# A feed-forward phase on one core: a bank copied for two late readers, last norm's weights loaded and used elsewhere, held sums ahead of the gated product

## What is computed

```python
def conv_ffn(x, w_up, ffn_conv_w, ffn_conv_b, w_down):
    u = causal_depthwise_conv(x @ w_up, ffn_conv_w, ffn_conv_b)   # width 3
    g = u[..., :D_FF]            # D_FF = 2816
    v = u[..., D_FF:]
    return (jax.nn.silu(g) * v) @ w_down

x = layer_norm(DEEPNORM_ALPHA * x + y, ln1_g[l], ln1_b[l])
y = conv_ffn(x, w_up[l], ffn_conv_w[l], ffn_conv_b[l], w_down[l])
x = layer_norm(DEEPNORM_ALPHA * x + y, ln2_g[l], ln2_b[l])
```

## Time and profile before

| what | value |
|---|---|
| median of 3 runs | 1924.68 us (1923.73 to 1924.71) |
| the profiled execution, time | 1924.79 us |
| the profiled execution, span | 1923.1 us, mean granted PE clock 0.990 |
| PE busy | 1869.6 us, 97% |
| DVE busy | 1472.9 us, 77% |
| ACT busy | 939.1 us, 49% |
| POOL busy | 213.5 us, 11% |
| DMA | 153 GB/s over the span |
| chain that ended last | PE 70%, DVE 8%, ACT 2%, DMA 2% |

### The profile page before, as it was taken

One profiled execution on the slowest core, in us unless ns is written; L12 is line 12 of the kernel. 1 busy time (PEld: TensorE's weight loads), 2 busy tenths in 40 slices (PEclk: granted clock), 3 DMA queues, 4 the chain that ended last, 5 costly groups with the idle time before them and its releaser, 6 DMA issues.

```text
span 1923.1 us, 26236 instructions
## 1 busy us (share of the span) xinstructions
PE 1869.6 (97%) x8722; PEld 1557.5 (81%) x8722; DVE 1472.9 (77%) x1931; ACT 939.1 (49%) x1598; POOL 213.5 (11%) x307
## 2 busy tenths in 40 slices
PE   7999999899999899999999999999999999999898
PEld 7888889688888688888888788888888787888786
DVE  6643238788988888888888988777878768658898
ACT  4211125756664656565656655555567335325221
POOL 1100032300000022222220020000000000000112
PEclk9999999999999999999999999999999999999999
DMA  6532234654436543434345433221225668557443
GB/s 230 186 110 72 71 113 157 210 178 157 160 129 218 216 143 131 149 124 153 122 151 184 144 133 110 76 87 76 88 76 170 231 215 290 185 186 272 174 171 114
DMA packets 171931, 296.13 MB, mean 154 GB/s; under 512 B 11728, under 2 KB 106192, under 8 KB 171856
## 3 DMA queue, kind: packets, MB, share of 16 engines
q1 hardware_dynamic: 171856, 295.18, 44.2%
HBM read 189.23 MB, written 105.91 MB: 153 GB/s over the span
## 4 chain that ended last, share of the span: by engine, by line
PE 70%; DVE 8%; ACT 2%; DMA 2%; issue 2%; SPq 0%; POOL 0%; DVEq 0%; ACTq 0%; POOLq 0%
PE banks L2241 19%; PE banks L2247 19%; PE banks L2244 19%; PE banks L1136 7%; DVE mov_lo L2454 3%; PE banks L1164 1%; PE banks L1118 1%; PE banks L1069 1%; DVE sta_lo L2450 1%; DMA y_scratch<-up_and_out 1%; DMA mov_raw<-x_operands 1%; ACT mov_hi L2318 1%; PE banks L1100 1%; DVE up_and_out L2488 1%; PE banks L1089 1%
## 5 line engine op out<-in xcount | busy, mean ns | idle before, releaser
L2241 PE MATMUL banks<-mov_hi,sta_hi 128*128 128x512 f32 x1848 | 502.8, 393 | 17.2 <-ACT half_sums L2331 5.9
L2247 PE MATMUL banks<-mov_lo,sta_hi 128*128 128x512 f32 x1848 | 499.5, 391 | 1.2 <-DVE mov_lo L2454 1.0
L2244 PE MATMUL banks<-mov_hi,sta_lo 128*128 128x512 f32 x1848 | 499.4, 391 | 0.0
L2241 PEld LDWEIGHTS banks<-mov_hi,sta_hi 128*128 128x128 f32 x1848 | 348.8, 189 | 94.8 <-ACT half_sums L2331 7.6
L2247 PEld LDWEIGHTS banks<-mov_lo,sta_hi 128*128 128x128 f32 x1848 | 348.0, 189 | 76.5 <-DVE mov_lo L2454 4.2
L2244 PEld LDWEIGHTS banks<-mov_hi,sta_lo 128*128 128x128 f32 x1848 | 349.3, 189 | 73.2
L2311 ACT ACTIVATE sta_hi<-sta_raw 128x512 fp32r<-128x512 f32 (+1 forms) x340 | 197.6, 611 | 134.0 <-PE banks L2247 96.3
L2450 DVE TENSOR_TENSOR sta_lo<-sta_raw,sta_hi 128x512 fp32r<-128x512 f32 (+1 forms) x340 | 223.0, 671 | 36.0 <-ACT sta_hi L2311 34.1
L2340 ACT ACTIVATE half_sums<-banks 128x512 f32<-128x512 f32 x68 | 40.7, 598 | 180.1 <-PE banks L2247 180.1
L288 PE MATMUL banks<-x0t_hi,win_hi 128*128 128x512 f32 x320 | 126.5, 395 | 0.0
L288 PE MATMUL banks<-x0t_hi,win_lo 128*128 128x512 f32 x320 | 124.8, 390 | 0.0
(11 more groups left out here) (244 smaller groups left out, 2650.6 us busy)
## 6 DMA issues: line engine op xcount, KB each, us to landing
sta_raw<-in_w_up SPq DMA_DIRECT2D x88, 512.0 KB, 4.1
hidden_scratch<-up_and_out SPq DMA_DIRECT2D x44, 512.0 KB, 2.6
y_scratch<-up_and_out SPq DMA_DIRECT2D x16, 1024.0 KB, 7.4
sta_raw<-hidden_scratch SPq DMA_DIRECT2D x32, 512.0 KB, 4.5
up_and_out<-y_scratch SPq DMA_DIRECT2D x16, 1024.0 KB, 4.9
x_operands<-x_operands_out SPq DMA_DIRECT2D x56, 256.0 KB, 4.2
mov_raw<-x_operands SPq DMA_DIRECT2D x14, 1024.0 KB, 7.7
mov_raw<-in_w_down SPq DMA_DIRECT2D x44, 256.0 KB, 4.7
```

The lines of the kernel that those rows point to most:

```text
L2241: pe.matmul(psum, sa_hi[j][:, k, :], mv_hi[j][:, k, :], start=(start and k == 0), stop=False, skip_group_check=True)
L2244: pe.matmul(psum, sa_lo[j][:, k, :], mv_hi[j][:, k, :], start=False, stop=False, skip_group_check=True)
L2247: last = pe.matmul(psum, sa_hi[j][:, k, :], mv_lo[j][:, k, :], start=False, stop=(stop and k == m - 1), skip_group_check=True)
```

## The change

It has five parts, which touch four engines.

- **The bank copied (`keep_first`, ACT and PE).** In blocks 0 and 44 ACT copies P1's bank 4 to bank 6, which nothing else uses there, before `keep_u4`. The c22 reader on DVE then reads bank 6, PE's P6 no longer waits for `c22`, and the copy is counted on `u4` (one more count after block 0, two more after block 44).
- **Held sums first (DVE).** At the openings of stages 1 and 2 `held_sums` of the next block comes ahead of `gated`, in stage 2 with the next `lo` of P1. In block 0 `held_sums(second)` and `lo(second, 1)` come ahead of the waits for the last stores, `clear_edge` and `up_c22(first)`.
- **Norm weights loaded earlier (SP).** In block 60 the two loads come ahead of the store of y of block 59 and of the load of y for block 61.
- **Norm weights used later (DVE).** `centred` is gone. `finish` does only `tile_stats`; `scaled` of both tiles comes ahead of `normalise`.
- **Counts.** The waits on `u4` go by `u4_count`.

```diff
+            act.wait_ge(x1t_out, 4 * NCH)
+            up.keep_first(first)
             up.keep_u4(first)
...
             up.moving_lo(0, 6)
+            up.held_sums(second)
+            up.lo(second, 1)
             dve.wait_ge(last_xt, 48)
             dve.wait_ge(x1_sums, 4 * NCH)
             up.clear_edge()
             up.up_c22(first)
-            up.held_sums(second)
-            for j in (1, 2, 3, 4):
+            for j in (2, 3, 4):
                 up.lo(second, j)
...
+    def kept(b):
+
+        return at(b, 0) or at(b, BASE[UP_STAGES])
+
+    def u4_count(b):
+        return num(b) + 2 + (b.st >= UP_STAGES)
...
             if before is not None and before.st < UP_STAGES:
                 store_hidden(before)
+            if opens(b) and b.st == LAST:
+                sp.wait_ge(mov_lo_ok, 7 * LAST + 5)
+                for n, v in enumerate((a["ln2_g"], a["ln2_b"])):
+                    sp.dma_start(g_b[:, n, :], v.rearrange("(o n) -> o n", o=1).to_broadcast((P, D))).then_inc(gb_loaded, 16)
             if b.st >= UP_STAGES:
...
                 if after is not None:
                     load_y(after)
-            if opens(b) and b.st == LAST:
-                sp.wait_ge(mov_lo_ok, 7 * LAST + 5)
-                for n, v in enumerate((a["ln2_g"], a["ln2_b"])):
-                    sp.dma_start(g_b[:, n, :], v.rearrange("(o n) -> o n", o=1).to_broadcast((P, D))).then_inc(gb_loaded, 16)
...
-            pe.wait_ge(u4, num(b) + 1)
+            pe.wait_ge(u4, u4_count(b))
             product(b, 5, y, False, True)
-            pe.wait_ge(c22, num(b) + 1)
+            if not kept(b):
+                pe.wait_ge(c22, num(b) + 1)
             product(b, 6, z, False, True)
...
+        def keep_first(b):
+
+            act.wait_ge(prod[1], num(b) + 1)
+            act.activation(ps[:, 6, :], ps[:, 4 + b.r, :], ACT.Copy).then_inc(u4, 1)
...
                 keep_u2(b)
+                if kept(b):
+                    keep_first(b)
...
         def down_c22_product(b):
             dve.wait_ge(y_in[b.r], (num(b) - BASE[UP_STAGES] - b.r) * 8 + 16)
-            dve.wait_ge(prod[1], num(b) + 1)
-            first_addend(b, 1, 1, ps[:, 4 + b.r, :]).then_inc(c22, 1)
+            if kept(b):
+                dve.wait_ge(u4, u4_count(b) - 1)
+            else:
+                dve.wait_ge(prod[1], num(b) + 1)
+            first_addend(b, 1, 1, ps[:, 6 if kept(b) else 4 + b.r, :]).then_inc(c22, 1)
...
             if b.st == LAST:
-                centred(b, 0)
+                tile_stats(b, 0)
             down_c21(b)
             if b.st == LAST:
-                centred(b, 1)
+                tile_stats(b, 1)
...
             if was_up and opens(b):
-                gated(before)
+                held_sums(after)
                 if b.st >= UP_STAGES:
+                    lo(after, 1)
+                    gated(before)
                     down_c22_product(b)
-                held_sums(after)
+                else:
+                    gated(before)
...
                 if opens(b):
-                    lo(after, 1)
+                    if was_down:
+                        lo(after, 1)
                 else:
                     down_c22_product(b)
                 if before.st == LAST:
+                    scaled(before, 0)
+                    scaled(before, 1)
                     normalise(before)
```

More of the change, by code:

```diff
@@ L1893 @@
 TensorOps = namedtuple("TensorOps", "open_banks product_0 product_1 products_2_3 rest stages")
-ScalarOps = namedtuple("ScalarOps", "hi moving_hi preset keep_u2 keep_u4 up_c11 stages")
+ScalarOps = namedtuple("ScalarOps", "hi moving_hi preset keep_u2 keep_first keep_u4 up_c11 stages")
 VectorOps = namedtuple("VectorOps", "lo moving_lo held_sums clear_edge up_c22 stages")
@@ L2291, in rest @@
             product_0(after)
-            pe.wait_ge(u4, 1)
+            pe.wait_ge(u4, u4_count(b))
             product(b, 5, y, False, True)
-            pe.wait_ge(c22, 1)
             product(b, 6, z, False, True)
@@ L2442, in stages @@
             walk(act, body)
-        return ScalarOps(hi, moving_hi, preset, keep_u2, keep_u4, up_c11, stages)
+        return ScalarOps(hi, moving_hi, preset, keep_u2, keep_first, keep_u4, up_c11, stages)
     def vector(dve):
@@ L2473, in up_c22 @@
         def up_c22(b):
-            dve.wait_ge(u4, num(b) + 1)
+            dve.wait_ge(u4, u4_count(b))
             if past(b, 1):
                 dve.wait_ge(conv_done[VALUE], num(b))
-            dve.tensor_tensor(tokens(b, VALUE, 1), bank(4 + b.r), u[:, 1, :].rearrange("p (q t) -> p q t", t=P), ALU.add).then_inc(c22, 1)
+            dve.tensor_tensor(tokens(b, VALUE, 1), bank(6 if kept(b) else 4 + b.r), u[:, 1, :].rearrange("p (q t) -> p q t", t=P), ALU.add).then_inc(c22, 1)
         def up_c21(b):
@@ L2557, in tile_stats @@
             dve.bn_aggr(lst[:, e, 12:14], lst[:, e, 0:12]).then_inc(ln_var, 1)
-        def centred(b, e):
-            tile_stats(b, e)
-            scaled(b, e)
         def scaled(b, e):
```

## The result

| | before | changed |
|---|---|---|
| median | 1924.7 us (1923.7 to 1925.5) | 1911.2 us (1909.9 to 1912.8) |
| ratio | | 0.9934, 95% interval 0.9922 to 0.9946 |
| profiled execution, time and span | 1924.8 and 1923.1 us | 1909.9 and 1908.2 us |
| granted PE clock, mean | 0.990 | 0.997 |

The account below looks back on a forecast made before the run. PE was busy for 97% of the span, so gains had to come from its idle time or clock. The terms 8.05 + 2.8 + 0 + 2.7 - 1.2 = 12.3 us gave 1912.4 us, range 1910.2 to 1917.2.

Parts of the forecast that it names:

- stage 4, P1 to P5 of block 61: Opening of stage 4: c21 of block 60 no longer waits for the weights, P5 of block 61 starts 8.05 us earlier.
- lateness of y: Load of y for block 61: lands 0.4 us before DVE needs it, cost 0; 1.5 us late would cost 1.2.
- block 0: Opening in block 0: P6 no longer waits for c22, and P6 of block 1 begins 2.8 us earlier.
- stage 1: Opening of stage 1: earlier held sums gain 0 at P6 of block 23, bounds -0.2 and +0.3 us.
- stage 2: Opening of stage 2: P6 of block 44 no longer waits for c22, P3 of block 45 starts 2.7 us earlier.
- clock: PE clock at the openings of block 0 and stages 1 and 2: -1.2 us for one fall, 0 to -6 for all.
- stage 3: Stage 3 was to keep its order, with no gain counted.
- only stage 4 counts: Rival: the copy does nothing in block 0 and stage 2; gain 8.05 us, 1916.6 us, chance 0.09.
- more than forecast: Rival: clock full everywhere and DVE reaches its lo parts earlier; gain 13.5 to 15 us, chance 0.10.

Follow-up runs that it names:

- e1: Changed kernel with only the stage 4 edits (norm weights loaded earlier and used later), without the bank copy and early held sums; 1915.6 us.
- e2: Changed kernel with only the bank copy and early held sums, the norm weights loaded and used as in the kernel before; 1918.9 us.
- e3: Changed kernel with the norm weights' loads put back behind the store and load of y, their late use kept; 1910.0 us.
- e7: Changed kernel with the gated product put back ahead of the held sums in stage 1 alone; 1911.9 us.
- e5: Changed kernel with the old order of held sums and lo restored in block 0 and stages 1 and 2, the copy kept; 1913.5 us.
- e6: Changed kernel without the bank copy, so P6 of blocks 0 and 44 waits for c22 again, held sums still early; 1922.6 us.
- e4: Changed kernel with each scaled operation put back right behind its tile's statistics, the norm weights still loaded early; 1912.0 us.
- e8: Changed kernel with c22 of blocks 1 and 23 moved ahead of the next block's two lo parts on DVE; 1909.4 us.
- e11: The changed kernel run once more, with no edit; 1912.0 us.

## Why the prediction was right, term by term

| term | forecast | measured | by |
|---|---|---|---|
| stage 4, P1 to P5 of block 61 | +8.05 | +8.05 | profile; e1 and e2 |
| lateness of y | 0 (1.2 for 1.5 late) | -0.20, and 0 to -1.5 in the other kernels | profile; e3, e7 |
| block 0 | +2.8 | +2.91 | profile; e2, e5, e6 |
| stage 1 | 0 (-0.2 to +0.3) | -0.28 | profile; e7 |
| stage 2 | +2.7 | +3.03 | profile; e2, e5, e6 |
| clock | -1.2 | 0 | profile; e3, e4, e8 |
| stage 3 | 0 | +0.22 | profile |
| sum | 12.3 | 13.7, and 1.15 in the mixing phase (13.5 by the medians) | |

The measured gain is 1.4 us over the sum, and 1.2 of that is the clock term, for a fall that didn't come; the other misses (+0.1, -0.3, +0.3, +0.2, -0.2) nearly cancel. The three large terms stand on mechanisms that the runs bear out. That the small ones cancel is luck.

**Stage 4.** The chain that I named (ln_b, `scaled`, c21, keep_u2, P4) was the one, and PE's length of five products the next limit. What I hadn't seen is that the two edits are two cures for one wait.

**y of block 61** is the term that I worked out wrong. I had the load of y issued at 1780.3 on before's clock; shifted by the 7.03 us that block 61 had come forward, 1773.3. It was issued at 1775.21. One part is that the store itself is issued 1.0 us later, behind two issues of SP that I put in the queue but not in SP's time (1770.42 - 7.03 = 1763.4, and 1764.42). The other is that the weights hold the store up by 3.4 us here (10.8 against 7.3), and over all the runs it lands in 10.6 to 12.1 against 7.3 to 8.8, not by the 2.5 that I had read from the order of landing, ln_b behind y. DVE was where I had it (1778.2; 1785.5 - 7.03 = 1778.5). The price of lateness was off the other way: I said that 1.5 us cost 1.2, and the first 1.9 cost nothing. I had the place wrong too: the lateness reaches PE at P1 of block 62 and not at the tail. The lag on DVE is made up faster than I reckoned: `scaled` no longer stands behind `bn_aggr`, and a block takes 18.49 us and not 18.88. From two starts of c12, five blocks apart:

```profile
1789.87 0.69 DVE L2518 TENSOR_TENSOR up_and_out<-up_and_out,banks 128x512 f32<-128x512 f32 x1
...
1882.31 0.68 DVE L2518 TENSOR_TENSOR up_and_out<-up_and_out,banks 128x512 f32<-128x512 f32 x1
```

**The clock** was a term of -1.2 for one fall in block 0 or stage 1. There was none in the changed kernel's profile, nor in e11's, but in three of the ten profiles with this opening there was. The error was less in the chance than in the price: I had a whole product at half clock, 2.6 us, of which 1.2 hides in the wait for c22. A fall took 1.1 us in block 0 (32.72 - 31.60) and 1.5 in stage 1 (425.72 - 424.24), and of these the wait hid all and 1.1 to 1.2; what remained was 0.3 to 0.5 us for both together.

**Block 0 and stage 2** held to 0.1 and 0.3 us. In stage 2 I had charged 0.36 us for the copy on ACT; the lo of block 45's P2 starts at 1494.91, which is 1498.69 on before's clock (P6 of block 23 had come forward by 3.78), and it was 1498.78: that delay didn't come. The rival "only stage 4 counts" would have made e2 no faster than before; e2 was 5.2 faster. **Stage 1**: the hidden store released ACT's first tap, as I said, and the sums' 1.1 us came to nothing. The -0.28 is just outside my bound of -0.2: the tap starts at 1076.83, on before's clock 1080.89 (P6 of block 1 had come forward by 4.06), 0.27 later than in the earlier trace rows.

The rival "more than forecast" (13.5 to 15) is nearest to the profiled execution; by the medians the time lies at its edge. Both of its reasons came true in part: the clock stayed full, and DVE came to the lo of block 45's P2 0.45 us earlier than I had it.

## What to carry to other kernels

Where PE waits for a chain through three engines, ask of every wait in the chain whether another edit already clears it: here the weights' load could have stayed where it was (DVE would have waited 0.27 us for it), and moving it ahead of a store put a new wait on the edge of the critical path. A buffer copy and an earlier order may each be worth little or be harmful alone (early sums without the copy lost 5.7 us in two openings) and be right together. And a wait that looks free in one profile should be compared over several executions: here 2.1 us cost 0.2, and 3.4 us cost 1.5.
